# A routed mixture of experts on one core: router logits from the raw x2, routing in two parts, and slot products tile by tile

## The reference, cut to what matters

```
x  = x + gate1 * (mixed @ w_o)
h2 = rms_norm(x, norm2_g) * (1 + scale2) + shift2      # scale2, shift2: one set for context, one for latent tokens
gl = h2 @ w_rg + b_rg                                  # 4 groups;  gp = softmax(gl), top 1
el = (h2 @ w_re + b_re).reshape(-1, 4, 4)              # 4 experts in each group, top 2 of the chosen group
combine = weight of the chosen group * normalised weight of its two experts
x  = x + gate2 * sum over the two experts of  combine * (silu(h2 @ w_gate) * (h2 @ w_up)) @ w_down
y  = rms_norm(x, norm_final_g)
```

## Time and profile before

| | |
|---|---|
| median of 3 runs | 739.93 us |
| profiled execution, first to last instruction | 737.5 us |
| PE busy | 703.8 us (95%) |
| DVE, ACT, POOL busy | 544.1, 344.3, 201.3 us |
| mean granted clock of PE | 0.982 |
| moved from and to HBM | 138.29 and 20.05 MB |

### The profile page before, as it was taken

How to read it: one execution, slowest core, us unless ns; L and a number is a source line. 1 busy time by engine, 2 the same in 40 slices (tenths; PEclk the granted TensorE clock), 3 DMA queues, 4 the chain that set the end, 5 groups by cost and what they waited for, 6 DMA issues and landing times.

```text
span 737.5 us, 11172 instructions
## 1 busy us (share of the span) xinstructions
PE 703.8 (95%) x4440; PEld 611.4 (83%) x4440; DVE 544.1 (74%) x785; ACT 344.3 (47%) x454; POOL 201.3 (27%) x84
## 2 busy tenths in 40 slices
PE   5899999999999999999999999998989999999985
PEld 2499999999998899999999998886368888877752
DVE  3547999999768765955556563555799999888877
ACT  4552223433333444446365121134387888777622
POOL 4004321322200000000000000000239999797560
PEclk9999999999999999999999999999599999999998
DMA  9954145445625345512325326266958999999783
GB/s 321 377 169 141 59 172 172 172 172 173 218 83 114 31 120 123 116 61 61 111 64 166 114 71 217 80 245 218 412 195 335 394 406 404 393 357 361 262 283 144
DMA packets 75607, 149.10 MB, mean 202 GB/s; under 512 B 11302, under 2 KB 54626, under 8 KB 68836
## 3 DMA queue, kind: packets, MB, share of 16 engines
q1 hardware_dynamic: 61572, 125.28, 49.4%
q10 hardware_dynamic: 10096, 12.63, 4.8%
q0 software_dynamic: 3888, 10.49, 4.2%
HBM read 138.29 MB, written 20.05 MB: 215 GB/s over the span
## 4 chain that ended last, share of the span: by engine, by line
PE 76%; DMA 9%; DVE 4%; issue 3%; ACT 3%; POOL 2%; SPq 2%; POOLq 0%; DVEq 0%; ACTq 0%
PE psum L990 36%; PE psum L1241 8%; PE psum L1283 7%; PE psum L505 3%; PE psum L925 3%; PE psum L506 3%; PE psum L511 3%; DMA down_raw<-in_w_e_down 2%; DMA w_more<-in_w_ada 2%; PE psum L1188 2%; DMA xg<-h_d,slot_b 1%; PE psum L1432 1%; SPq L791 1%; PE psum L1118 1%; PE psum L1009 1%
## 5 line engine op out<-in xcount | busy, mean ns | idle before, releaser
L990 PE MATMUL psum<-hh,w_h 128*128 128x320 f32 x608 | 144.4, 319 | 0.2 <-issue 0.2
L990 PE MATMUL psum<-hh,w_l 128*128 128x320 f32 x608 | 138.5, 309 | 0.0
L990 PE MATMUL psum<-hl,w_h 128*128 128x320 f32 x608 | 138.4, 309 | 0.0
L2014 DVE SCALAR_TENSOR_TENSOR psum<-conv,taps,psum 128x760 f32<-128x760 f32 x103 | 104.5, 1015 | 3.5
L990 PEld LDWEIGHTS psum<-hh,w_h 128*128 128x128 f32 x608 | 99.8, 188 | 5.4 <-issue 3.1
L990 PEld LDWEIGHTS psum<-hl,w_h 128*128 128x128 f32 x608 | 101.6, 188 | 0.0
L990 PEld LDWEIGHTS psum<-hh,w_l 128*128 128x128 f32 x608 | 101.5, 188 | 0.0
L717 POOL TENSOR_TENSOR down_l<-down_raw,down_h 128x2048 fp32r<-128x2048 f32 x16 | 87.8, 5486 | 20.8 <-ACT down_h L1787 20.3
L683 POOL TENSOR_TENSOR ob<-obh,toff 128x260 bf16<-128x260 f32 x1 | 2.0, 1995 | 332.1 <-DVE obh L591 332.1
L2300 DVE TENSOR_TENSOR w_l<-w_raw,w_h 128x2048 fp32r<-128x2048 f32 x26 | 77.0, 2966 | 11.7 <-ACT w_h L1793 11.7
L917 POOL TENSOR_TENSOR w_l<-w_raw,w_h 128x2048 fp32r<-128x2048 f32 x9 | 41.8, 4640 | 144.1 <-ACT w_h L1468 144.1
(11 more groups left out here) (384 smaller groups left out, 1403.4 us busy)
## 6 DMA issues: line engine op xcount, KB each, us to landing
w_raw<-in_w_in SPq DMA_DIRECT2D x20, 1024.0 KB, 6.7
down_raw<-in_w_e_down SPq DMA_DIRECT2D x17, 1024.0 KB, 12.3
w_raw<-in_w_ada SPq DMA_DIRECT2D x16, 1024.0 KB, 9.2
w_raw<-in_w_e_gate SPq DMA_DIRECT2D x13, 1024.0 KB, 7.8
w_raw<-in_w_e_up SPq DMA_DIRECT2D x13, 1024.0 KB, 11.3
w_more<-in_w_ada SPq DMA_DIRECT2D x8, 1024.0 KB, 10.5
y_d<-yy ACTq DMA_DIRECT2D x15, 512.0 KB, 8.2
y_d<-in_x_sample SPq DMA_DIRECT2D x12, 512.0 KB, 8.1
```

What stands on the lines that cost most here:

```text
L990: mm = pe.matmul(psum[:, p + q, 0:HALF], w, r[:, k, q * HALF:(q + 1) * HALF], start=(k == 0 and x == 0), stop=(k == KT - 1 and x == 2))
L2014: ins = dve.scalar_tensor_tensor(out=after, in0=src, scalar=w, in1=before, op0=MUL, op1=ADD)
```

## The change

It does these things:

- **Logits from raw x2.** Instead of h2, PE turns x2 itself (`turn_x2`, columns 512q+k in steps of 4), and the router weights are scaled by norm2_g(1+scale2) beforehand (`wrs`). The inverse norm is multiplied in at the end (`scaled_logits`) and the constant from shift2 (`shift_terms`, `shift_rows`, `lgc`) is added. Four small column loads and split loads of the router weights join SP's queue.
- **Turns inside wo.** `turn_x2(t-1)` stands inside tile t of the second half (behind its fifth of eight steps), the left half of tile 4 inside tile 4, and `logits(t-1)` behind tile t. Only `logits(3)`, `logits(4)` and the right half of tile 4 come behind the last tile.
- **h2 in one pass.** `x2 * scale` is made on POOL for the left columns of all tiles and for both halves of two tiles, and by `h2_right` on DVE else. One fused DVE pass (`h2_rows`) does the rest.
- **Two parts of routing.** Tiles 0 and 1 are ranked and counted during wo, tiles 2 to 4 behind it. `choose` ranks by comparing pairs (15 sets of 16 differences) in place of three successive maxima. The positions are formed of the chosen entries alone.
- **Slot list tile by tile.** `oav` holds token numbers in place of ones, so one product of `oav` and `obh` per tile and choice gives `slot_i` without the steps behind it. PE starts on tiles as DVE finishes them.
- **Order.** The last tile of h2 is stored by POOL. The first gather must land before the second is issued. SP's order changes: down weights of slot 0 behind the last logits, then gate and up of slot 2, down of 2, and down of 1 only behind `row_weights` of slot 0. The load of `gfb` moves to slot 2. In slot 0 PE does the 16 high products, then `row_weights`, then turns slot 1's rows, then the 8 low ones. `gate2_spread(1)` stands between the turn of slot 0's rows and slot 0. `late_tables` moves on DVE from before slot 0 to behind slot 0. The silu table is loaded ahead. `gate2_products` 1 to 3 get four filler matmuls each.

The core of the diff (address constants, semaphore aliases, and the numerics of the ranking are left out):

```diff
-    def h2_out(act, t):
+    def x2_out(act, t, q):
         if t >= 2:
             act.wait_ge(lgt_pe, t - 1)
...
+    def scaled_logits(dve, then, t0, t1):
+        for t in range(t0, t1):
+            dve.wait_ge(h2_rstd, t + 1)
+            ins = dve.scalar_tensor_tensor(out=lg[:, t, :], in0=psum[:, 7, LG_AT[t]:LG_AT[t] + 20],
+                                           scalar=rms[:, 24 + t:25 + t], in1=lgc[:, min(t, 1), :], op0=MUL, op1=ADD)
...
+    def places_of(dve, t):
+        for i in range(2):
+            ins = dve.tensor_scalar(oav[:, i, t, :], iota[:, :], place_in[:, i, t:t + 1], tokval[:, t:t + 1],
+                                    ALU.is_equal, MUL)
...
+    def slot_table(dve):
+        dve.wait_ge(rt_pe, 3)
+        dve.tensor_scalar(slot_i[:, :], psum[:, 6, 0:NS], float(EMPTY * P), None, ADD).then_inc(slots, 1)
...
     def experts_pool(pool):
+        pool.wait_ge(mod_in, 16 * 6)
+        for t in range(NT):
+            pool.wait_ge(x2_left, X2_LEFT + t + 1)
+            pool.tensor_tensor(h2[:, t, 0:512], x2[:, t, 0:512], bsc[:, min(t, 1), 0:512], MUL).then_inc(h2_half, 1)
...
+        pool.wait_ge(h2_dve, NT)
+        pool.dma_start(h2_d[(NT - 1) * P:NT * P, :], h2[:, NT - 1, :]).then_inc(h2_last_st, 16)
+        pool.wait_ge(h2_last_st, 16)
+        pool.wait_ge(h2_st, 16 * NT)
         pool.wait_ge(slots, 1)
...
-        for b in range(3):
+        known_gather(0)
+        pool.wait_ge(xg_in[0], 16)
+        for b in range(1, 3):
             known_gather(b)
...
         gate2_unit(3)
+        h2_store(3)
         gate_up(1, 1, own(1))
-        for t in range(3, NT):
-            h2_store(t)
+        sp.wait_ge(lg_done, 2)
+        down_weights(0, 0, own(0))
         gate_up(2, 0, own(2))
-        sp.wait_ge(x2_done, NT)
+        sp.wait_ge(h2_st, 16 * NT)
+        sp.wait_ge(h2_last_st, 16)
+        down_weights(2, 0, own(2))
+        sp.wait_ge(rt_pe, 4)
         down_weights(1, 1, own(1))
-        sp.wait_ge(lg_done, 1)
-        down_weights(0, 0, own(0))
-        sp.wait_ge(h2_st, 16 * (NT + 1))
-        down_weights(2, 0, own(2))
         gate_up(3, 1, own(3))
...
+                    if half and t and k == 4:
+                        turn_x2(t - 1, 0)
+                        turn_x2(t - 1, 1)
+                    if half and t == NT - 1 and k == 2:
+                        early_counts()
+                    if half and t == NT - 1 and k == 6:
+                        turn_x2(t, 0)
...
+        gate2_products(0)
+        turn_x2(4, 1)
+        for t in range(ROUTED, NT):
+            token_logits(t, stop=(t < NT - 1))
...
+        gate2_products(1)
+        late_counts()
+        gate2_products(2)
+        pe.wait_ge(hots, 1)
         for t in range(NT):
...
+            for i in range(2):
+                mm = pe.matmul(psum[:, 6, 0:NS], oav[:, i, t, :], obh[:, i, t, :], start=(t == 0 and i == 0),
+                               stop=(t == NT - 1 and i == 1))
...
+            if first:
+                pe.wait_ge(e_hi, 2)
+                for k in range(KT):
+                    if k % 4 == 0:
+                        pe.wait_ge(x_lo, k // 4 + 1)
+                    for x in (xh, xl):
+                        pe.matmul(psum[:, s, :], x[:, s, k, :], both(wh, k), start=(k == 0 and x is xh), stop=False)
+                row_weights()
+                turn_x(1 - s, u + s, b + 1)
...
+        pe.wait_ge(slots, 1)
+        pe.wait_ge(z_free, len(TILES) + 2)
+        gate2_spread(0)
+        keep_clock(4, 2)
         turn_x(0, 0, 0)
+        gate2_spread(1)
...
+        def h2_rows(t):
...
+            dve.scalar_tensor_tensor(out=h2[:, t, :], in0=h2[:, t, :], scalar=rms[:, 24 + t:25 + t], in1=bsh[:, min(t, 1), :],
+                                     op0=MUL, op1=ADD).then_inc(h2_dve, 1)
...
             if not last:
                 w_lo(1 - s, b + 1, 1)
+            if isinstance(b, int) and b == 0:
+                late_tables(dve, then)
```

More of the change, by code:

```diff
@@ L1259, in logits, with shift_terms @@
+        def logits(t, ks=range(KT)):
+            pe.wait_ge(h2_ev, 2 * t + 1 + (len(ks) == KT))
             if t:
                 pe.wait_ge(lgt_done, t)
+            for k in ks:
+                rows = slice(GRP * (k % NGRP), GRP * (k % NGRP + 1))
+                mm = pe.matmul(psum[rows, 4, 0:P], wrs[:, min(t, 1), k, :], h2t[:, t % 2, k, :], start=(k < NGRP),
+                               stop=(k >= len(ks) - NGRP))
+            mm.then_inc(lgt_pe, 1)
+        def shift_terms():
+            pe.wait_ge(wrs_done, WRS_DONE)
@@ new lines, in late_counts @@
+        def late_counts():
+            pe.wait_ge(picked, 2)
+            late = NT - ROUTED
+            cols = lambda n, m: psum[:, 7, LATE_COUNTS + n * NE:LATE_COUNTS + m * NE]
+            spread = lambda one, n: one.unsqueeze(1).to_broadcast([P, n, NE])
+            pe.matmul(cols(0, late + 1), onesb[:, :], spread(picksum[:, :], late + 1), start=True, stop=False)
+            for n in range(late):
+                pe.matmul(cols(n + 1, late + 1), onesb[:, :], spread(picks[:, ROUTED + n, :], late - n), start=False, stop=False)
+            for n in range(late):
+                mm = pe.matmul(cols(n, n + 1), upper[:, :], picks[:, ROUTED + n, :], start=False, stop=(n == late - 1))
+            mm.then_inc(rt_pe, 1)
@@ L1374, in down, with row_weights @@
             mm.then_inc(e_used, 1)
+        def row_weights():
+            pe.wait_ge(hots, 2)
+            for n in range(2 * NT):
+                mm = pe.matmul(psum[:, 6, 4 * NS:7 * NS], oa[:, n // NT, n % NT, :], obw[:, :, n, :],
+                               start=(n == 0), stop=(n == 2 * NT - 1))
+            mm.then_inc(rt_pe, 1)
         def slot(b, s, u, first=False, last=False):
@@ L1379, in slot @@
                 turn_act(b - 1, isinstance(b, int) and b == 1)
-            if not last:
+            if not (first or last):
                 turn_x(1 - s, u + s, b + 1)
@@ L1863, in _ @@
             x_high(0, 0, q, True)
+        for v in range(2):
+            gate2_out(v)
         def slot(b, s, u, last=False):
@@ L1873, in slot @@
                 store_y(s, b - 2)
+            if isinstance(b, int) and b == 2:
+                act.wait_ge(tables, 1)
+                act.dma_start(gfb[:, :], a["norm_final_g"].rearrange("(o n) -> o n", o=1).to_broadcast([P, D])).then_inc(gate2_in, 16)
             if not last:
@@ L2284, in _ @@
                 late_low("wo", 3)
[L2286 to L2295 removed]
+        dve.wait_ge(late_in, 16 * 6)
@@ L2297, in w_lo @@
+        add_mixed(2 * NT - 1)
+        h2_right(NT - 1)
+        x2_inverse(NT - 1)
+        for t in range(ROUTED):
+            places_of(dve, t)
         def w_lo(s, b, c):
@@ L2329, in _ @@
         slot_weights(dve, then)
-        for c in range(2):
-            w_lo(0, 0, c)
+        w_lo(0, 0, 0)
         x_low(0, 0, 0)
         x_low(0, 0, 1)
-        late_tables(dve, then)
+        w_lo(0, 0, 1)
+        weight_table(dve, then)
         def one_hots(last):
```

482 lines of the change are left out of this document (304 added, 178 removed).

## The result

The changed kernel takes 753.64 us, the median of four runs (751.01 to 756.45), beside 739.74 us (737.07 to 741.36, four runs) for the kernel before on the same chip: a ratio of 1.0192, 95% interval 1.0164 to 1.022. Slower by 13.9 us, and outside the predicted range. The profiled execution took 751.01 us with a span of 749.1, so its own difference to the span before, 737.5, is 11.6 us; it is the fastest of the four.

A forecast was written before the change was run, and what follows sets the result against it. PE, DMA, DVE and POOL were taken as nearly full in the slots, so only the stretch before them could shrink. Terms +4.5 - 7.5 + 3.8 + 1.5 - 2.0 = +0.3 us gave 740.2 us, range 734.5 to 745.0.

The forecast's parts named there:

- Step 1: wo stage, up to its last product (T): inserted transposes, logits and small products lengthen PE's work by 4.5 us.
- routing ahead might stall PE: wo stage: DVE waiting for PE's counts between tiles would add 1 to 2 us, within the forecast's range.
- Step 2: From T, the last wo product's end, to the slot list: ready at T + 15.8 in place of T + 25.7, gain 9.9 us.
- step 3: Slot list to gathered rows: POOL's own store, then a gather of 8.2 us; rows at T + 25, gain so far 7.1.
- Steps 3 and 4: Slot list through gather and turn into slot 0: slot 0 starts at T + 27.7 in place of T + 35.2, gain 7.5.
- held-store rival: Before the first gather: POOL's store lands after T + 16.8, gain only 2.2, 744.5 us; chance 0.22 together with low clock.
- Step 5: Slot 0 to slot 1: later row turn and ACT's weights make act ready at +10.5 us, PE idles; price +3.8 us.
- clock rival: Slot 0: low clock lasts into its 16 products, up to +3.8 us on the forecast; chance 0.22 together with held store.
- Step 6: late_tables on DVE behind slot 0: 2.8 us of work with 1 us of slack, cost +1.5 us, bounds 0 and 2.8.
- Step 7: Slots 8 to 14: DMA gets ahead during earlier delays, giving back -2.0 us net, bounds 0 and -3.4.

The follow-up runs named there:

- e12: e9 with the transposes of x2's tiles 0 to 3 made twice in the second half of the wo stage; ratio 1.0115 to the kernel before.
- e9: e5 with ACT's high weights of slot 1 ahead of slot 0's rows and SP's down(0) and gate_up(2) loads held behind the gathers; 742.74 us, ratio 1.0042.
- e1: Changed kernel with late_tables moved on DVE from behind slot 0 to before the low parts of slot 0's rows; ratio 1.0110 to the kernel before.
- e4: Changed kernel with the last h2 tile stored by SP in place of POOL; ratio 1.0117 to the kernel before.
- e2: Changed kernel with ACT's high parts of slot 1's weights moved before the copies of slot 0's rows; ratio 1.0176 to the kernel before.
- e7: e6 with SP's down(0) loads held until the first gather landed and slot 2's weights until the second; 746.02 us, ratio 1.0088.
- e3: Changed kernel with slot 2's gate and up loads held back until the first gather has landed; ratio 1.0145 to the kernel before.
- e11: Kernel before with slot 1's rows turned behind slot 0's 16 high products, not before the 24; ratio 1.0070 to the kernel before.
- e5: e1 with 12 unused filler matmuls in PE's gap between slots 0 and 1; 744.01 us, ratio 1.0066 to the kernel before.
- e6: e5 with e2's edit and DVE's act(0) before both low parts of slot 1's weights; 746.14 us, ratio 1.0083 to the kernel before.
- e8: Kernel before with late_tables alone moved on DVE behind slot 0; ratio 1.0084 to the kernel before, 6.2 us slower.
- e10: e5 with e7's change of SP's queue, ACT's order as in the changed kernel; 742.80 us, ratio 1.0035 to the kernel before.

## Why the prediction was wrong

The two traces differ by 11.6 us where my sum said 0.3. By my own steps:

**Step 1, the wo stage: +5.8 in place of +4.5.** The kind of cost was right (e12), the size not. I summed durations of the inserted instructions and left out that each insertion also breaks a row of products. The timeline of PE after, from the last product before an insertion:

```profile
487.28 0.39 PE L1431 MATMUL psum<-w_h,ml 128*128 128x512 f32 x1
487.51 1.12 PE L1028 MATMUL psum<-ident,x 128*128 128x128 f32 x8
488.38 0.48 PE L1431 MATMUL psum<-w_h,mh 128*128 128x512 f32 x1
488.70 0.40 PE L1431 MATMUL psum<-w_l,mh 128*128 128x512 f32 x1
```

Products follow each other every 0.23 us; the eight transposes take 0.87, and the product behind them keeps its successor off for 0.32. With some nine more breaks than before and a few products at 0.235 behind each, that makes about 1 us, by my estimate. My guess that routing ahead might stall PE did not come true: it was never idle there.

**Step 2, the slot list: T + 17.8 in place of T + 15.8.** "PE and the second-gate work fit beside it" was wrong by 2 us, which in the end cost nothing, as step 3 shows. The timeline after:

```profile
525.50 0.22 PE L1412 MATMUL psum<-picks,upper 128*128 128x16 bf16 x3
...
525.83 0.32 DVE L613 TENSOR_TENSOR tq<-chosen,psum 128x48 f32<-128x48 f32 x2 [2.04 <-PE psum L1412]
...
531.57 0.18 DVE L672 TENSOR_SCALAR slot_i<-psum 128x26 int32<-128x26 f32 x1 [0.27 <-PE psum L1487]
```

DVE waited 2.04 us for the late counts, which on PE stand behind the second gate's products and their fillers, and these ran at the low clock (window 520 to 522 above). In e9 the clock stayed at 1.00 there, and the same wait was 0.56 us:

```profile
522.98 0.32 DVE L613 TENSOR_TENSOR tq<-chosen,psum 128x48 f32<-128x48 f32 x2 [0.56 <-PE psum L1414]
```

There the list was ready at T + 16.3, as in e1 to e4, which have after's order on PE and DVE up to the list; so 1.5 of the 2 us come and go with the clock from run to run.

**Steps 3 and 4, to slot 0: T + 30.3 in place of T + 27.7.** Of these 2.6 us, 2.1 are the gather's late start, T + 18.9 in place of the T + 16.8 that my sum implies, and the term that failed is the landing of POOL's own store. It was issued at T + 9.6 (I had 9.3), took 8.45 us and landed at T + 18.0, 0.3 us behind the list. I had given it T + 13 to T + 22 and then counted it as if it were in time. The late list was not the cause: in e1 and e2 the list was ready at T + 16.3 and the gather still left at T + 18.9 and T + 19.0. So by my own condition, a landing after T + 16.8, the held-store rival had begun to hold, though far from its 10.8 us. Holding back loads made the store 7.1 to 7.3 us (e7, e9), and the gather left at T + 17.6 to T + 17.7. The other terms came out: the gather took 8.49 us (I had 8.2), the way from the turn to slot 0's first product 2.9 (2.7). The reason given for 8.2, the backlog, is shown by e3 and e9. The Trainium skill's rule weighed there ("DMA: Bandwidth & Descriptors", SWDGE vs HWDGE vs iDMA), by which the DMA engines take turns between the queues, did not keep the gather out of SP's backlog: 8.49 us beside it, 4.79 without it (e3).

**Step 5, slot 0 to slot 1: +6.2 in place of +3.8**, counted from slot 0's start to the end of slot 1's products (13.66 us before, 19.82 after). The mechanism was right: `act` 10.2 us behind slot 0's start, predicted 10.5, and e11 shows it alone. What failed is the sentence "PE idles for it" with no price on the idle time. It put slot 1 at the low clock; e5 measures this part at 2.6 us. My clock rival had looked for the low clock in slot 0, for PE's wait before it, and there the clock held in this run; it fell there in e1, e2 and e6.

**Step 6, `late_tables`: +4.7 in place of +1.5, over my upper bound of 2.8.** This is the largest miss. I bounded the move by the time the same instructions took at their old place, where POOL was idle. At the new place POOL works on its low part of the down weights, and a DVE step of two tiles in SBUF lasted until POOL's instruction had ended. One step grew by 4.4 us (0.17 to 4.57), and the delay made a low part of slot 2's weights meet POOL's next instruction in turn: 6.29 us in place of 2.28, ending 2.2 us behind POOL. Slot 1 to 2 took 3.0 us more than before, slot 2 to 3 took 1.6 more. e1 takes the cost away and e8 brings it into the kernel before. The Trainium skill ("SBUF — State Buffer", Who interferes with whom) says that DVE and GpSimd (POOL) share one port pair under an exclusive lock, that a DVE instruction with two SBUF inputs contends for it with a GpSimd instruction that reads SBUF, and that the order of issue decides which of the two is blocked. This trace agrees: POOL began 0.9 us before the step, which took 4.57 us in place of 0.17. My had POOL at 49.12 of 50 us, which was the warning: there is little time in a slot when a small step on DVE would not meet it.

**Step 7, given back at the end: -0.2 us in slots 3 to 14, where I had -2.0 by the end.** In the slots, where I had placed it, the credit did not come. e9 and e10 point the other way: slots that start sooner lose 2 to 3 us again before slot 14. The 2.5 us that after's profile has less behind slot 14 are within what that stretch varies by (55.7 to 58.6 us in these runs).

Misses of 1.3, 2.6, 2.4, 3.2 and -0.7 us in these steps (the last is -2.7 us, with the stretch behind slot 14, against -2.0), and 2.6 us in the stretch ahead of the wo stage, which no step can claim, make up the distance from 0.3 to 11.6. Measured singly, the parts give +5.8 for the wo stage, -4.9 to slot 0's start, +6.2 (e8) and +5.2 (e11), together +12.3 us, beside 13.9 by the medians (interval 12.1 to 16.3). This is an estimate and no proof, as it adds medians and single profiles, and e8's two figures alone lie 3 us apart.

I had counted each move beside the resource it uses, and not beside what runs there at the same time. The two largest misses, the tables and the low clock of slot 1, are second costs of moves that I had listed rightly.

**What stays open.** Why the medians are 13.9 us apart where the two traces show 9.0 from the wo stage on, in the fastest of after's four executions; why the store takes 7 us even with loads held back; why e9's slots 1 to 14 take 3 us more than before's, with the same pace of 9.34 us in the middle; and how much of the wo stage's 5.8 us could be had back by putting insertions together, which was not tried.

## What to carry to other kernels

When an instruction is moved, price it at its new place: look up which engine works beside it there, and if that is POOL, take what is left of POOL's instruction as the price of any DVE step with two SBUF operands, however small. When the start of a transfer hangs on several waits, place each of them: an earlier list was worth nothing as long as the store landed after it. When a move makes PE wait a few microseconds, add the price of the low clock on what follows, and try a filler before taking the order apart. A latency gained ahead of a loop counts only if what is paid for it (here 5.8 us of PE work in full) is less, and this sum can be made from the trace before anything else.

## What the runs showed of the hardware that was not expected

- A DVE sum of two 128 x 16 tiles took 4.57 us (after), and one of 10 columns 4.61 us (e8), each until POOL's instruction of 5.3 to 5.4 us ended; alone they take 0.17 to 0.18. A DVE instruction of 2.28 us that began beside POOL's took 6.29 us (after) and 5.35 us (e8), ending 2.2 us behind POOL's in both; two of them took 8.92 us together (e6).
- With PE's order behind T the same, the clock differed between runs: 0.50 in the window 520 to 522 of after and 518 to 520 of e5, 1.00 throughout in e9. A wait of DVE for PE went from 0.56 to 2.05 us with it.
- PE idle for 3.50 us before slot 1 (after, e1, e4) or 4.70 us (e11) was followed by some 3 to 6 us at 0.50, though PE was busy again at once; with twelve filler products there the clock stayed at 1.00 (e5). Before slot 0 it fell after 4.39 us (e1), 4.03 us (e2) and 2.40 us (e6) idle, and held after 2.14 us (after), 2.44 us (e5) and 2.90 us (e4), so the length of the gap alone does not tell.
- The same gather took 8.49 us with SP's loads queued beside it and 4.79 us without (e3). A store took 8.45 us from POOL's queue (after), 7.35 from SP's (e4), and still 7.1 from POOL's with slot 0's down weights and slot 2's loads held back (e9).
- A transpose put between products cost 0.12 us where its own slot in a row of eight is 0.109, and the break of the row 0.09 us more (0.32 in place of 0.23).
